# SSD scan of a hybrid layer: chunks of 128 tokens with carried states instead of decayed scores between all token blocks

## The reference

```python
xdt = xh * dt[..., None]
a = dt * a_neg
a_cs = jnp.cumsum(a.reshape(bsz, n_c, SSM_CHUNK, heads), axis=2)
decay_in = segsum_exp(a_cs.transpose(0, 1, 3, 2))
scores = jnp.einsum("bclhn,bcshn->bchls", cc, bc) * decay_in
y_diag = jnp.einsum("bchls,bcshp->bclhp", scores, xc)
decay_to_end = jnp.exp(a_cs[:, :, -1:, :] - a_cs)
chunk_states = jnp.einsum("bclhn,bclhp->bchpn", bc * decay_to_end[..., None], xc)
chunk_decay = jnp.exp(a_cs[:, :, -1, :])
...
    return state * d_c[..., None, None] + s_c, state
...
y_off = jnp.einsum("bclhn,bchpn->bclhp", cc, prev) * jnp.exp(a_cs)[..., None]
```

## Time and profile before

| | |
|---|---|
| median of 3 runs | 1640.26 us (1638.53 to 1642.61) |
| the profiled execution | 1639.5 us |
| its span, first to last instruction | 1637.7 us |
| mean granted TensorE clock | 0.992 |
| TensorE busy | 1599.6 us, 98% |
| VectorE busy | 722.5 us, 44% |
| ACT busy | 546.7 us, 33% |
| POOL busy | 529.6 us, 32% |

### The profile page before, as it was taken

One profiled execution on the slowest core, in us unless ns is written; L12 is line 12 of the kernel. 1 busy time (PEld: TensorE's weight loads), 2 busy tenths in 40 slices (PEclk: granted clock), 3 DMA queues, 4 the chain that ended last, 5 costly groups with the idle time before them and its releaser, 6 DMA issues.

```text
span 1637.7 us, 20044 instructions
## 1 busy us (share of the span) xinstructions
PE 1599.6 (98%) x7674; PEld 1321.5 (81%) x7674; DVE 722.5 (44%) x902; ACT 546.7 (33%) x810; POOL 529.6 (32%) x458
## 2 busy tenths in 40 slices
PE   7999999999999999999999998999999999999998
PEld 7878888888888888888886667788888888888886
DVE  4342544447544333322455658664435543333223
ACT  4322332223532222212454465322225422222121
POOL 2870001310188068286112504385001881000000
PEclk9999999999999999999999998999999999999999
DMA  6533122222554354344131111244222453332331
GB/s 195 171 113 102 52 78 53 77 77 77 155 147 141 97 151 141 105 157 152 53 116 52 52 52 52 71 148 123 96 101 77 133 152 102 102 89 91 102 116 51
DMA packets 189296, 170.89 MB, mean 104 GB/s; under 512 B 20656, under 2 KB 161968, under 8 KB 189232
## 3 DMA queue, kind: packets, MB, share of 16 engines
q1 hardware_dynamic: 181168, 144.84, 29.3%
q0 software_dynamic: 8064, 25.20, 5.0%
HBM read 167.91 MB, written 2.10 MB: 104 GB/s over the span
## 4 chain that ended last, share of the span: by engine, by line
PE 90%; DVE 5%; ACT 2%; issue 1%; POOL 1%; DMA 0%; DVEq 0%; SPq 0%; ACTq 0%; POOLq 0%
PE bank L1551 28%; PE bank L1552 27%; PE bank L1553 27%; PE bank L1757 1%; PE bank L1773 1%; PE bank L1849 1%; PE bank L1825 1%; PE bank L1677 1%; DVE w_lo L1091 1%; PE bank L1765 1%; POOL inv_rms L642 1%; DVE decay L1457 0%; PE bank L1718 0%; PE bank L1793 0%; PE bank L1835 0%
## 5 line engine op out<-in xcount | busy, mean ns | idle before, releaser
L1551 PE MATMUL bank<-h_hi,w_hi 128*128 128x512 f32 (+1 forms) x1504 | 577.3, 384 | 4.1 <-DVE h_lo L1119 1.6
L1552 PE MATMUL bank<-h_lo,w_hi 128*128 128x512 f32 (+1 forms) x1504 | 562.1, 374 | 0.0
L1553 PE MATMUL bank<-h_hi,w_lo 128*128 128x512 f32 (+1 forms) x1504 | 561.9, 374 | 0.0
L1091 DVE TENSOR_TENSOR w_lo<-raw,w_hi 128x2048 fp32r<-128x2048 f32 (+1 forms) x146 | 307.2, 2105 | 315.5 <-ACT w_hi L773 315.2
L1551 PEld LDWEIGHTS bank<-h_hi,w_hi 128*128 128x128 f32 x1504 | 286.2, 190 | 66.2 <-issue 14.3
L1553 PEld LDWEIGHTS bank<-h_hi,w_lo 128*128 128x128 f32 x1504 | 285.7, 190 | 50.1
L1552 PEld LDWEIGHTS bank<-h_lo,w_hi 128*128 128x128 f32 x1504 | 286.0, 190 | 48.0 <-issue 1.9
L773 ACT CAST w_hi<-raw 128x2048 fp32r<-128x2048 f32 (+1 forms) x146 | 244.1, 1672 | 216.5 <-PE bank L1553 216.4
L692 POOL TENSOR_SCALAR mod_raw<-mod_raw,c_silu 128x512 f32<-128x512 f32 x96 | 183.7, 1914 | 46.2 <-DMA mod_raw<-in_mod_w 42.6
L695 POOL TENSOR_TENSOR mod_acc<-mod_acc,mod_raw 128x512 f32<-128x512 f32 x96 | 145.5, 1515 | 8.2
L1551 PE MATMUL bank<-w_hi,act_hi 128*128 128x512 f32 x352 | 137.9, 392 | 0.0
(11 more groups left out here) (300 smaller groups left out, 1778.4 us busy)
## 6 DMA issues: line engine op xcount, KB each, us to landing
raw<-in_w_in SPq DMA_DIRECT2D x102, 512.0 KB, 4.5
mod_raw<-in_mod_w POOLq DMA_DIRECT2D x96, 256.0 KB, 3.2
raw<-in_w_ffn_in SPq DMA_DIRECT2D x44, 512.0 KB, 4.9
raw<-in_w_gate SPq DMA_DIRECT2D x22, 512.0 KB, 4.1
raw<-in_w_up SPq DMA_DIRECT2D x22, 512.0 KB, 5.3
raw<-in_w_down SPq DMA_DIRECT2D x20, 512.0 KB, 4.3
raw<-in_w_ffn_out SPq DMA_DIRECT2D x20, 512.0 KB, 4.4
raw<-in_w_out SPq DMA_DIRECT2D x8, 512.0 KB, 4.4
```

The source lines that it names most:

```text
L1091: ins = dve.tensor_tensor(w_lo[s][:, cols], raw[s][:, cols], w_hi[s][:, cols].bitcast(F32), ALU.subtract)
L1551: pe.matmul(o, st_hi, mv_hi, start=first, stop=False)
L1552: pe.matmul(o, st_hi, mv_lo, start=False, stop=False)
L1553: return pe.matmul(o, st_lo, mv_hi, start=False, stop=last)
```

## The change

The scan works on four chunks of 128 tokens. Inside a chunk the decayed scores are made for the 128x128 diagonal block only, so a head has one item of 512 columns (four blocks side by side) instead of four tasks. dt is multiplied into the scores, not into xs. What comes from earlier chunks goes through a state of 64 x 64 per head at the start of chunks 1 to 3: B (turned) times xs weighted by dt and the decay to the chunk's end gives the chunk states; VectorE carries them on; C, multiplied by the exponential of the sum from the chunk's start, reads them. Heads go in the order 0, 4, 1, 5, ..., one of each group. xs, the weighted xs, B, C and the states are all split into halves. POOL makes no low halves any more. Cut to its core (the rest is buffers, semaphores and selectors):

```diff
@@ POOL
+            gp.tensor_tensor(start_sel[:], ident[:, 64:64 + HEADS], ident[:, 96:96 + HEADS], ALU.add)
...
+            then(gp.tensor_tensor(group_sel[0:HEADS, :], eye[:, :, 0], eye[:, :, 1], ALU.add))
...
-                    gp.tensor_tensor(g_lo[:, cols], decay[j][:], g_hi[:, cols].bitcast(F32), ALU.subtract).then_inc(g_wide_lo, 1)
...
+            for t in (bt_hi, bt_lo):
+                ins = gp.memset(t[:].bitcast(F32), 0.0)
+            for n, c in enumerate(SSD_PAIRS):
+                gp.wait_ge(y_gated, n + 1)
                 gp.tensor_tensor(z_t[:, c, :], y_ssm[:, c, :], y_ssm[:, c, :], ALU.mult).then_inc(sq_done, 1)
@@ ACT, attention
+                if s == 3:
+                    act.wait_ge(row_apart, 1)
+                    act.activation(to_end[:], to_end[:], ACT.Exp)
+                    act.activation(from_start[:], from_start[:], ACT.Exp).then_inc(row_exp, 1)
@@ ACT, scan
+            def decays(i):
+                act.wait_ge(dec_ready, i + 1)
+                wait(act, ys_done, i - 2)
+                for j, cols in enumerate(CHUNKS):
+                    o = HEADS * j + SSD_HEADS[i]
+                    ins = act.activation(decay[i % 3][:, cols], bank[:, dec_bank(i), cols], ACT.Exp, bias=nacs_col[:, o:o + 1])
+                ins.then_inc(dec_done, 1)
...
+            for j in range(NT):
+                act.copy(xs_hi[:, j, :], bank[:, 4 + j, :]).then_inc(xs_hi_done, 1)
+            for j in range(NT - 1):
+                act.copy(xw_hi[:, j, :], xw_tmp[:, j, :]).then_inc(xw_hi_done, 1)
...
+            for i in range(1, len(SSD_HEADS) + 1):
+                if i < len(SSD_HEADS):
+                    if i % 2 == 0:
+                        c_hi_part(i // 2)
+                    decays(i)
+                g_hi_part(i - 1)
+                if i in (3, 4):
+                    split(n_mg, part=i - 3)
@@ VectorE, rows
-            dve.tensor_tensor_scan(rb, rb, rb, 0.0, ALU.add, ALU.bypass).then_inc(row_ready, 1)
+            then(dve.tensor_tensor_scan(rb, rb, rb, 0.0, ALU.add, ALU.bypass))
+            for j in range(NT - 1):
+                end = rb[:, P * j + P - 1:P * j + P]
+                dve.tensor_scalar(to_end[:, CHUNKS[j]], rb[:, CHUNKS[j]], -1.0, end, ALU.mult, ALU.add)
+                ins = dve.tensor_scalar(from_start[:, CHUNKS[j]], rb[:, CHUNKS[j + 1]], end, None, ALU.subtract)
+            ins.then_inc(row_apart, 1)
             split(n_x + 1)
@@ VectorE, scan
+            def scores(i):
+                dve.wait_ge(dec_done, i + 1)
+                for j, cols in enumerate(CHUNKS):
+                    o = HEADS * j + SSD_HEADS[i]
+                    d = decay[i % 3][:, cols]
+                    ins = dve.scalar_tensor_tensor(d, d, dt_col[:, o:o + 1], cb[:, i % 2, cols], ALU.mult, ALU.mult)
+                ins.then_inc(g_ready, 1)
...
+                dve.tensor_tensor(g_lo[i % 3][:], decay[i % 3][:], g_hi[:, i % 2, :].bitcast(F32), ALU.subtract).then_inc(g_lo_done, 1)
...
-                then(dve.scalar_tensor_tensor(y_ssm[rows, c, :], xs_t[rows, c, :], d_col[rows, c:c + 1], o[0:SSM_HD, :],
-                                              ALU.mult, ALU.add))
-                dve.tensor_tensor(y_ssm[rows, c, :], y_ssm[rows, c, :], o[SSM_HD:P, :], ALU.add).then_inc(y_head, 1)
+                dve.scalar_tensor_tensor(y_ssm[rows, c, :], xs_t[rows, c, :], d_col[rows, c:c + 1], bank[0:SSM_HD, 6 + i % 2, :],
+                                         ALU.mult, ALU.add).then_inc(y_head, 1)
...
+            for c in (1, 2):
+                then(dve.tensor_tensor(by_quad(states[c][:]), by_quad(was),
+                                       whole_col[:, 4 * c - 4:4 * c].unsqueeze(2).broadcast_to([P, 4, SSM_HD]), ALU.mult))
+                dve.tensor_tensor(states[c][:], states[c][:], added, ALU.add).then_inc(state_ready, 1)
...
+            for i in range(1, len(SSD_HEADS) + 1):
+                if i < len(SSD_HEADS):
+                    if i % 2 == 0:
+                        c_product(i // 2)
+                    scores(i)
+                    if i % 2 == 0:
+                        c_lo_part(i // 2)
+                g_lo_part(i - 1)
+                if i in (5, 6):
+                    split(n_mg, part=i - 5)
+                if i > 2:
+                    finish_head(i - 3)
+                if i in (5, 6):
+                    finish_pair(i - 5)
@@ TensorE
+            pe.wait_ge(row_w_ready, 2)
+            for j in range(NT - 1):
+                pe.transpose(bank[:, 5, o:o + HEADS], to_end[:, CHUNKS[j]], ident[0:HEADS, 0:HEADS])
...
+            def decay_rows(i):
+                o = bank[:, dec_bank(i), :]
+                wait_item(3 * (i // 2) + i % 2 - 1)
+                pe.matmul(o, head_row(SSD_HEADS[i]), a_rows[:], start=True, stop=False)
+                pe.matmul(o, ident_r[:], mask_st[:].unsqueeze(1).broadcast_to([P, NT, P]), start=False, stop=True).then_inc(dec_ready, 1)
+            def head_products(i):
...
+                for j, cols in enumerate(CHUNKS):
+                    pe.matmul(o, xs_hi[:, j, xc], hi, start=True, stop=False)
+                    pe.matmul(o, xs_hi[:, j, xc], lo, start=False, stop=False)
+                    ins = pe.matmul(o, xs_lo[:, j, xc], hi, start=False, stop=j == 0)
+                    if j > 0:
+                        hi, lo = (c[st_rows, q % 2, CHUNKS[j - 1]] for c in (c_hi, c_lo))
+                        pe.matmul(o, states_hi[j - 1][st_rows, sc], hi, start=False, stop=False)
+                        pe.matmul(o, states_hi[j - 1][st_rows, sc], lo, start=False, stop=False)
+                        ins = pe.matmul(o, states_lo[j - 1][st_rows, sc], hi, start=False, stop=True)
+                ins.then_inc(ys_done, 1)
...
+            filler(5)
+            for j in range(NT - 1):
+                ins = pe.transpose(bank[:, 4, CHUNKS[j]], xs_t[:, 4, CHUNKS[j]], ident[:])
...
+            for g in range(2):
+                for cols in CHUNKS:
+                    ins = pe.matmul(bank[:, 5 + g, cols], xs_t[rows, 4, cols], xs_t[rows, 5, cols], start=True, stop=True)
...
+            filler(4)
...
+            c_rows_of(0)
+            decay_rows(0)
...
+            for c in range(NT - 1):
+                for g in range(2):
+                    ins = three_passes(bank[:, 6 + c // 2, 256 * (c % 2):256 * (c % 2) + 256], bt_hi[:, c, g, :], bt_lo[:, c, g, :],
+                                       xw_hi[:, c, xc], xw_lo[:, c, xc], g == 0, g == 1)
...
+            filler(5)
+            for i in range(1, len(SSD_HEADS) + 2):
+                if i < len(SSD_HEADS):
+                    if i % 2 == 0:
+                        c_rows_of(i // 2)
+                    decay_rows(i)
+                filler(2)
+                if i >= 2:
+                    head_products(i - 2)
```

More of the change, by code:

```diff
@@ new lines, in head_cols, with c_selector @@
+            def head_cols(col, j):
+                return col[:, HEADS * j:HEADS * j + HEADS].unsqueeze(2).broadcast_to([P, HEADS, SSM_HD])
+            def c_selector(q):
+                heads = start_sel[:, :].rearrange("p (g q) -> p g q", q=4)[:, :, q:q + 1]
+                dve.tensor_copy(c_sel[:, q % 3, :].rearrange("p (g n) -> p g n", g=2),
+                                heads.bitcast(F32).broadcast_to([P, 2, SSM_HD])).then_inc(c_sel_done, 1)
+            for q in range(3):
+                c_selector(q)
@@ L1470, in _ @@
-            narrow_lo(len(SSD_TASKS) - 1)
-            finish_head(HEADS - 1)
-            finish_pair(3)
+            c_product(0)
+            split(n_sc + 2, part=0)
+            c_lo_part(0)
+            dve.wait_ge(cb_done, 2)
+            scores(0)
+            dve.wait_ge(states_in, 2)
+            state_lo_part(0, bank[:, 6, 0:256])
+            for c in (1, 2):
+                was = bank[:, 6, 0:256] if c == 1 else states[1][:]
+                added = bank[:, 6, 256:512] if c == 1 else bank[:, 7, 0:256]
+                then(dve.tensor_tensor(by_quad(states[c][:]), by_quad(was),
+                                       whole_col[:, 4 * c - 4:4 * c].unsqueeze(2).broadcast_to([P, 4, SSM_HD]), ALU.mult))
+                dve.tensor_tensor(states[c][:], states[c][:], added, ALU.add).then_inc(state_ready, 1)
+                dve.wait_ge(state_ready, c)
@@ L1474, in _ @@
+            for i in range(len(SSD_HEADS) - 2, len(SSD_HEADS)):
+                finish_head(i)
+                finish_pair(i - 4)
             take(n_sc + 2, 1, sc_raw[:, 5, PAD:PAD + TOK])
@@ L1853, in _ @@
                         eighth(r)
[L1854 removed]
+            pe.wait_ge(row_apart, 1)
             for r, row in ((0, row_a), (1, row_b)):
@@ L1869, in _ @@
                 ins.then_inc(xs_turned, 1)
-            for s in range(8):
-                g, j = divmod(s, NT)
-                rows = slice(SSM_HD * g, SSM_HD * g + SSM_HD)
-                if s < 4:
-                    pe.wait_ge(xdt_done, s + 1)
-                else:
-                    pe.wait_ge(cb_done, s - 3)
```

(19 more changed lines are left out.)

274 lines of the change are left out of this document (165 added, 109 removed).

## The result

| | before | after |
|---|---|---|
| median of the runs | 1640.00 us | 1629.16 us (1628.98 to 1630.86) |
| span of the profiled execution | 1637.7 us | 1627.2 us |
| mean granted TensorE clock | 0.992 | 0.995 |

(1640.00 is the median of four runs of the kernel before; the 1640.26 further up was that of the first three.) The ratio of the two kernels is 0.9938, with a 95% interval of [0.9925, 0.9951]: 10.8 us or 0.6% faster, more than the 0.3% that a measurement tells apart. The forecast was 1624.5 us, range 1615 to 1634. The time lies in the range, 4.7 us above the forecast and just outside the band 1621 to 1629 that belonged to the mechanism forecast.

What follows compares the result with a forecast made beforehand. TensorE was taken as the bound, busy 98% of the span, with 20 of the scan's 67 us not work. Scan -14.7, clock behind it -2.0, additions ahead +1.3 and +0.4 took 1639.5 to 1624.5 us, range 1615 to 1634.

Steps and rivals of the forecast that it cites:

- mechanism forecast: Whole kernel: the change works as reckoned, 1624.5 us, band 1621 to 1629; chance 0.50.
- Output products: TensorE in the scan: a head's 21 matmuls with their weight-shape changes take 2.3 us, bounds 1.6 and 3.3.
- Rival A: Scan products: changes between 128x64 and 64x64 cost nothing, a head takes 1.6 us, time 1620; chance 0.20.
- B: Scan products: the small matmuls go at 0.11 us each, 8 us more in all, time 1632.5; chance 0.15.
- A's outer end of 1615: Scan: shape changes free and VectorE's waits in turns 4 to 6 vanish as well, time 1615.
- the walk over VectorE in turns 6 to 8: Scan: g_lo times followed turn by turn against TensorE's demand; cover thin in turns 6 to 8, 1 us of waits.
- the 1 us allowed for waits: Scan: TensorE's waits from thin g_lo cover in turns 6 to 8, put at 1 us in the stage's end, 1018.8.
- Ahead of the scan: Before the scan: six VectorE row operations add 1.3 us (bounds 0 and 1.5), small transposes and matmuls 0.4.
- Clock: TensorE clock stays at 1.00 without gaps of 2 us; gate unit behind the scan 11.0 instead of 13.0 us.
- Rival C: Scan: a head's chain of engine steps, 6.1 us, is not overlapped and the clock falls, time 1645; chance 0.06.
- Rival D: Scan: the decayed scores saved were not what the stage waited for, little gained, 1634 to 1640; chance 0.09.

Runs made afterwards that it cites:

- experiment 8: Kernel before the change, with the low halves g_lo that POOL made now made by VectorE: 1633.75 us, ratio 0.9969.
- experiment 3: Changed kernel with a head's twelve chunk products before its nine state products, three weight-shape changes instead of seven, output not the scan's: 1628.12 us, ratio 0.9930.
- experiment 6: Joined kernel with a head's products reordered, three changes between the two weight shapes instead of five: 1622.93 us, ratio 0.9908.
- experiment 9: Joined kernel with the two kinds of product alternating, 17 weight-shape changes in a head instead of 5: 1652.13 us, ratio 1.0076.
- joined kernel: Changed kernel with row operations two tasks later, outputs taken before the next scores, three filler parts in turn 7, one in turn 9: 1623.54 us, ratio 0.9910.
- second profile: The changed kernel itself, nothing edited, measured and profiled once more: 1629.42 us, ratio 0.9940.
- experiment 1: Changed kernel with VectorE's output add of the head three back, and gating multiply, before a turn's score multiplies: 1627.64 us, ratio 0.9928.
- experiment 10: Joined kernel with output products one turn behind the decay rows instead of two, the 32 filler parts kept: 1641.50 us, ratio 1.0009.
- experiment 4: Changed kernel with two filler parts moved from turns 8 and 9 into turn 7: 1626.02 us, ratio 0.9930.
- experiment 5: The joined kernel: changed kernel with later row operations, outputs taken earlier and three filler parts in turn 7, one in turn 9: 1623.54 us, ratio 0.9910.

## Why the prediction was right, and where it was not

**Direction and mechanism: right, the size of the saving too large.** 10.8 us were saved, forecast 15.0. The score work fell, four round trips a head became one, the 10.3 us of waits for g_lo went, VectorE got its undisturbed prices (684 ns for 512 columns; forecast 690), and all later stages moved by what the scan saved. Only about half of the scan's gain is the chunked order's own, though: experiment 8 gets 5.3 us by taking g_lo off POOL.

**Output products: price right, a size slightly off.** A head was put at 2.3 us: 1.26, six times 0.14, and 0.19 out. It is 1.26 + 5 x 0.14 + 0.19 = 2.15 where the first load is done ahead (2.07 to the next matmul, and the 0.1 behind that one), and 2.3 where it waits for g_lo. The price of a change, read from attention, fits the one from 128x64 to 64x64 that no row had shown, but partly by luck: the row that it was read from is the entry into a 64-wide shape, and in the scan the entry itself costs nothing when g_lo is there. Attention's products are plain f32 between fp32r ones, the scan's are fp32r like their neighbours; whether that is the difference was not tested. In "TensorEngine Tiling (Array Packing)", Key Properties, the Trainium skill says that a change of tiling mode drains TensorE; the trace agrees for every change between 128 and 64 rows (experiments 3, 6 and 9 scale with their number), and does not show it for the entry from 128x128 to 128x64, a change of columns alone. The 81 ns of the Trainium skill, "TensorE: Matmul & The Clock Gate", Back-to-back issue gap, is not what this stream does: 0.06. Rival A (changes free) and B (0.11 each) fall. A's outer end of 1615 does not follow from its own terms either: eight times 0.7 and the 1.0 of waits give 1618.

**The step that failed: the walk over VectorE in turns 6 to 8.** It put g_lo of head 5 at 1008.0 against a demand at 1008.1 and called the cover thin, which was right: counted from the first transposes it forecast 41.5 against 41.6 us and measured were 41.3 against 41.0, a miss of 0.3 us. But it asked of the products only for g_lo. They also need the old output of the bank taken, and in VectorE's order that stands behind the split. So the 1 us allowed for waits became 2.4, and "the clock should stay at 1.00" cost 2.6 more. The joined kernel shows both: 50.4 us without them, against 51.3 of work in the forecast. So TensorE's work had been put 0.9 too high, mostly for the entries, and this hid a part of the miss: the forecast for the whole stage was 52.3, 1.9 above the joined kernel's and 3.1 below the changed one's.

**Ahead of the scan: half.** The wait for `sp_lo` grew to 1.69 us, forecast "about 1.6", and the small transposes cost the 0.4. The clock behind that wait (1.6) was not in the sum. In the second profile it did not fall there, and 109.8 - 108.1 = 1.7 is what was forecast.

**Clock: the rule in the prediction was wrong.** "Without gaps of 2 us it should stay at 1.00" is refuted by experiments 1 (0.81 us) and 9 (none). Its saving behind the scan was right in the first profile (1.9), and 1.5 of it was given back in the second. One line priced "if the clock falls once after all, 2 us come back"; every one of the thirteen profiles has at least one between attention and the gate units, so that line belonged in the sum.

**Rival C** was rightly small: it needed the chain uncovered, and experiment 10 shows what keeps it covered: with one turn the time is 1641.5, 3.5 below its 1645. **Rival D** was wrong: the waits went. But the prediction's reading that VectorE was slow because it met POOL is borne out (1148 against 418 ns), and POOL's share as a whole, hop and company together, is 5.3 of the 16 us of waits and clock.

## What to carry to other kernels

When a consumer's start is forecast, list all that it waits for, the release of its output buffer too, and find each of them in the producing engine's queue. An operation that frees a buffer goes ahead of work without a date (a weight split), and filler goes into the turn whose cover is thin: these two moves and the one of the rows gave 5.6 us, half as much again as the change. And shape changes of the weights are worth grouping only as long as the other engines' results come in time: experiments 3 and 6 took 4.6 and 2.3 us out of TensorE's work and shortened the scan by 2.0 and 0.7. In this kernel the next thing to try would be the order on ACT and VectorE in the even turns, where each waits for the other.

## What the runs showed of the hardware

The granted clock is not a function of one wait. At 2.4 GHz before, it fell to 1.2 at or behind every one of the ten waits of 2.1 us or more between attention and the gate units. Behind 1.7 us it fell in three profiles of six, behind 0.81 us in experiment 1, and not behind 1.02 and 0.76 us in experiment 4 or 1.22 in experiment 6. It fell with TensorE busy throughout, behind 17 shape changes in a head, and in ten of thirteen profiles near the 32 one-column matmuls of the norm behind the scan, as in the last row of experiment 5. A single fall cost about 1.5 us, the longer ones behind the waits of 2.4 us 2.6. What decides it is not settled; that it varies between executions of one kernel is shown. Ranges should hold one or two such falls.

A change between 128 and 64 contracted rows cost 0.14 us each time at full clock, over 17 changes in a head as well. The entry from 128x128 into 128x64 cost nothing (0.22 between starts) where the first weight load was done ahead, and 0.09 and the 0.05 behind it where that load had waited for g_lo.

VectorE's multiply and subtraction of two operands in SBUF got slower beside POOL (1148 and 731 ns for 256 columns, 418 alone), its operation with one operand in PSUM did not (742 and 741).
